# Split-weight matmuls of a two-layer decoder step: moving operands read backwards, weight rows of 136 columns, activation tiles at one offset from the weights

## What is computed

```python
def trunk_layer(x, ...):
    h = rmsnorm(x, norm1)
    qa, ka, va, hb, gate_b, gate_c, qc, fc, ic, og, zg = split_in(h @ w_in)   # 1024 -> 6400
    ya = dilated attention(rope(qa), rope(ka), va)      # six heads, three windows
    yb = gate_b * short convolution(gate_c * hb)
    yc = HGRN2 recurrence(qc, fc, ic), normed, times silu(og)
    g = sigmoid(zg + b_gate)
    mix = g[0] * (ya @ w_pa) + g[1] * (yb @ w_pb) + g[2] * (yc @ w_pc)
    x = x + mix @ w_o                                   # 1024 -> 1024
    h2 = rmsnorm(x, norm2)
    return x + square(relu(h2 @ w_up)) @ w_down, states # 1024 -> 4096 -> 1024
```

## Time and profile before

| | us |
|---|---|
| median of 3 runs | 812.23 (811.56 to 812.31) |
| span of the profiled execution, first to last instruction | 809.8 |
| TensorE matmuls busy | 801.3 (99%) |
| TensorE weight loads busy | 789.7 (98%) |
| VectorE busy | 570.3 (70%) |
| ScalarE busy | 439.6 (54%) |
| GpSimd busy | 274.7 (34%) |
| DMA packets, share of 16 engines (q1) | 72.3% |

### The profile page before, as it was taken

How to read it: one execution, slowest core, us unless ns; L and a number is a source line. 1 busy time by engine, 2 the same in 40 slices (tenths; PEclk the granted TensorE clock), 3 DMA queues, 4 the chain that set the end, 5 groups by cost and what they waited for, 6 DMA issues and landing times.

```text
span 809.8 us, 17686 instructions
## 1 busy us (share of the span) xinstructions
PE 801.3 (99%) x6786; PEld 789.7 (98%) x6786; DVE 570.3 (70%) x774; ACT 439.6 (54%) x627; POOL 274.7 (34%) x246
## 2 busy tenths in 40 slices
PE   8999999999999999999999999999999999999996
PEld 8999999999999999999999999999999999999996
DVE  6978898577877665545577788966797666645552
ACT  6663667545557664444354637674455666644442
POOL 3599293055700000122149827702663000001220
PEclk9999999999999999999999999999999999999998
DMA  8797779868567688777558968986765767787751
GB/s 327 226 342 279 279 236 328 229 226 314 185 208 226 215 287 285 257 239 250 190 179 225 359 244 289 278 254 232 271 225 178 247 235 250 240 285 241 253 207 53
DMA packets 125721, 199.88 MB, mean 247 GB/s; under 512 B 19680, under 2 KB 115376, under 8 KB 118192
## 3 DMA queue, kind: packets, MB, share of 16 engines
q1 hardware_dynamic: 124368, 196.48, 72.3%
q10 hardware_dynamic: 1296, 2.61, 0.9%
HBM read 191.17 MB, written 51.90 MB: 300 GB/s over the span
## 4 chain that ended last, share of the span: by engine, by line
PE 98%; DVE 1%; DMA 1%; ACT 0%; DVEq 0%; ACTq 0%; issue 0%
PE main L695 29%; PE main L696 28%; PE main L697 28%; PE small L697 1%; PE small L696 1%; PE small L695 1%; PE small L711 1%; PE small L740 1%; PE small L754 1%; DMA raw<-in_w_in 1%; PE main L680 1%; PE main L681 0%; PE main L684 0%; PE small L792 0%; PE main L671 0%; PE small L928 0%
## 5 line engine op out<-in xcount | busy, mean ns | idle before, releaser
L1043 ACT ACTIVATE w_hi<-raw 128x1024 fp32r<-128x1024 f32 (+1 forms) x256 | 266.4, 1043 | 234.3 <-PE main L697 148.6
L1292 DVE TENSOR_TENSOR w_lo<-raw,w_hi 128x1024 fp32r<-128x1024 f32 (+1 forms) x256 | 340.8, 1332 | 65.5 <-ACT w_hi L1043 64.5
L695 PE MATMUL main<-h_hi,w_hi 128*128 128x264 f32 x1248 | 357.9, 287 | 0.0
L696 PE MATMUL main<-h_lo,w_hi 128*128 128x264 f32 x1248 | 354.0, 284 | 0.0
L697 PE MATMUL main<-h_hi,w_lo 128*128 128x264 f32 x1248 | 353.9, 284 | 0.0
L695 PEld LDWEIGHTS main<-h_hi,w_hi 128*128 128x128 f32 x1248 | 235.3, 189 | 3.0 <-DVE w_lo L1292 1.5
L696 PEld LDWEIGHTS main<-h_lo,w_hi 128*128 128x128 f32 x1248 | 235.5, 189 | 0.1
L697 PEld LDWEIGHTS main<-h_hi,w_lo 128*128 128x128 f32 x1248 | 234.2, 188 | 0.0
L695 PE MATMUL main<-a_hi,w_hi 128*128 128x264 f32 x512 | 145.4, 284 | 0.0
L697 PE MATMUL main<-a_hi,w_lo 128*128 128x264 f32 x512 | 145.2, 284 | 0.0
L696 PE MATMUL main<-a_lo,w_hi 128*128 128x264 f32 x512 | 145.2, 284 | 0.0
(11 more groups left out here) (241 smaller groups left out, 1042.5 us busy)
## 6 DMA issues: line engine op xcount, KB each, us to landing
raw<-in_w_in SPq DMA_DIRECT2D x48, 1024.0 KB, 6.3
raw<-in_w_up SPq DMA_DIRECT2D x32, 1024.0 KB, 5.3
raw<-in_w_down SPq DMA_DIRECT2D x32, 1024.0 KB, 5.4
out_kvs<-in_cache SPq DMA_DIRECT2D x48, 512.0 KB
out_kvs<-in_cache SPq DMA_DIRECT2D x32, 496.0 KB
raw<-in_w_o SPq DMA_DIRECT2D x8, 1024.0 KB, 6.0
raw<-in_w_br SPq DMA_DIRECT2D x8, 768.0 KB, 4.8
gates<-q_scratch SPq DMA_DIRECT2D x4, 768.0 KB, 7.9
```

The lines of the kernel that those rows point to most:

```text
L695: pe.matmul(out[:, 0:TOK], wh, rh, start=start and k == 0, stop=False)
L696: pe.matmul(out[:, 0:TOK], wh, rl, start=False, stop=False)
L1043: act.activation(w_hi[:, slot(l, u), 0:k, :], raw_of(u, k), ACT.Copy).then_inc(w_hi_ready, 1)
L1292: dve.tensor_tensor(w_lo[:, slot(l, u), 0:k, :], raw_of(u, k), w_hi[:, slot(l, u), 0:k, :].bitcast(F32), ALU.subtract).then_inc(w_lo_ready, 1)
```

## The change

A helper `product` is put in place of `pe.matmul` in `first_units`, `unit_lo_last` and `unit`. It gives the same matmul with the moving operand's 264 columns from the last to the first and, so that the result lands where it did, the output's columns from the last to the first as well. The weights are loaded as before. Every block of `w_hi` and `w_lo` gets a row of 136 columns (544 bytes, of which 128 columns are used), so that its address moves on by 32 modulo 256 with each `k`, as the activations' does. Unused tiles (`before_h`, `before_gates`, `before_y_hi`, `before_y_lo`) put all activation tiles of the products (`h`, `mix`, `a`, `y`) at 64 modulo 256, which is 192 bytes on from the weights' 128. To make room, three small tiles that lay side by side share columns on different partitions (`sample_heads`). No instruction is added, dropped or moved, on any engine; operands and addresses differ.

```diff
+LINE = 8
-        w_hi = sb("w_hi", [P, RING, KT, P], F32R)
-        w_lo = sb("w_lo", [P, RING, KT, P], F32R)
+        w_hi_rows = sb("w_hi_rows", [P, RING, KT, P + LINE], F32R)
+        w_lo_rows = sb("w_lo_rows", [P, RING, KT, P + LINE], F32R)
         x = sb("x", [P, KT, TOK])
+        sb("before_h", [P, 6 * LINE])
         h_hi = sb("h_hi", [P, KT, TOK], F32R)
...
+        sb("before_gates", [P, 7 * LINE])
...
-            kv_s = sb("kv_s", [SAMPLES, NG, 2, P], stack=early)
-            q_s = sb("q_s", [SAMPLES, NG, P], stack=early)
+            sample_heads = sb("sample_heads", [P, NG * 2 * P], stack=early)
...
-            v_s = sb("v_s", [SAMPLES, 2, P], stack=early)
...
+            sb("before_y_hi", [P, 4 * LINE], stack=early)
             y_hi = sb("y_hi", [P, BT, TOK], F32R, stack=early)
+            sb("before_y_lo", [P, 2 * LINE], stack=early)
             y_lo = sb("y_lo", [P, BT, TOK], F32R, stack=early)
...
+        w_hi, w_lo = (t[:, :, :, 0:P] for t in (w_hi_rows, w_lo_rows))
+        kv_s = sample_heads[0:SAMPLES, :].rearrange("p (g k c) -> p g k c", g=NG, k=2)
+        v_s = sample_heads[32:32 + SAMPLES, 0:2 * P].rearrange("p (a c) -> p a c", a=2)
+        q_s = sample_heads[64:64 + SAMPLES, 0:NG * P].rearrange("p (g c) -> p g c", g=NG)
...
+            def product(out, w, rhs, start, stop):
+
+                return pe.matmul(out[:, TOK - 1::-1], w, rhs[:, ::-1], start=start, stop=stop)
...
-                    pe.matmul(out[:, 0:TOK], wh, rh, start=start and k == 0, stop=False)
-                    pe.matmul(out[:, 0:TOK], wh, rl, start=False, stop=False)
-                    last = pe.matmul(out[:, 0:TOK], wl, rh, start=False, stop=stop and k == nk - 1)
+                    product(out, wh, rh, start and k == 0, False)
+                    product(out, wh, rl, False, False)
+                    last = product(out, wl, rh, False, stop and k == nk - 1)
```

More of the change, by code:

```diff
@@ L665, in first_units @@
                         for u in us:
-                            pe.matmul(main[u][:, 0:TOK], w_hi[:, u, k, :], h_hi[:, k, :], start=k == 0, stop=False)
-                            pe.matmul(main[u][:, 0:TOK], w_hi[:, u, k, :], h_lo[:, k, :], start=False, stop=False)
+                            product(main[u], w_hi[:, u, k, :], h_hi[:, k, :], k == 0, False)
+                            product(main[u], w_hi[:, u, k, :], h_lo[:, k, :], False, False)
                     pe.wait_ge(piece_lo, i + 1)
@@ L670, in first_units @@
                         for k in ks:
-                            mm = pe.matmul(main[u][:, 0:TOK], w_lo[:, u, k, :], h_hi[:, k, :], start=False,
-                                           stop=k == KT - 1)
+                            mm = product(main[u], w_lo[:, u, k, :], h_hi[:, k, :], False, k == KT - 1)
                         if k == KT - 1:
@@ L679, in unit_lo_last @@
                 for k in range(KT):
-                    pe.matmul(out[:, 0:TOK], w_hi[:, u % RING, k, :], h_hi[:, k, :], start=k == 0, stop=False)
-                    pe.matmul(out[:, 0:TOK], w_hi[:, u % RING, k, :], h_lo[:, k, :], start=False, stop=False)
+                    product(out, w_hi[:, u % RING, k, :], h_hi[:, k, :], k == 0, False)
+                    product(out, w_hi[:, u % RING, k, :], h_lo[:, k, :], False, False)
                 pe.wait_ge(w_lo_ready, u + 5)
                 for k in range(KT):
-                    last = pe.matmul(out[:, 0:TOK], w_lo[:, u % RING, k, :], h_hi[:, k, :], start=False,
-                                     stop=k == KT - 1)
+                    last = product(out, w_lo[:, u % RING, k, :], h_hi[:, k, :], False, k == KT - 1)
                 return last
```

## The result

The change makes the kernel slower: 816.37 us in the median of five runs (815.77 to 816.70) against 811.84 for the kernel before on the same chip, a ratio of 1.0053 with a 95% interval of 1.0041 to 1.0066. The profiled execution spans 814.6 us, 4.8 more than before. The forecast was 783.

The account below looks back on a forecast made before the run. TensorE was taken as the bound, matmul count times distance. 32.7 us gained less 4 given back is 28.7; span 809.8 - 28.7 = 781.1, plus 2.4 for the median gives 783.5, say 783 us; range 762 to 814.

Parts of the forecast that it names:

- The bound: Whole kernel: TensorE busy 801.3 of 809.8 us, so time is the matmul count times the distance between starts.
- the 8.3 ns: Each split matmul: 120.8 ns less 112.5 for the stream, read as two on-chip memory reads getting in each other's way.
- Rows 6 and 7: Profile rows of weight loads beside one-column matmuls (about 110 ns each) and plain float32 matmuls of 264 columns (222.5 ns).
- the sum's term 6048 x (120.8 - 115.4) = 32.7 us: All matmuls but the first four units' 96: distance falls from 120.8 to 115.4 ns, saving 32.7 us.
- The rival "nothing": All matmuls: excess is a price of fp32r beside a weight load, same for any address; 812 us, chance 0.12.
- the 26 cycles: Each split matmul's cost beyond its 264 columns: 10.8 ns, 66 us over 6144 matmuls.
- The count of meetings: Moving read against weight load: 6.1 meetings per matmul at 1.36 ns now, 2.1 after, 2.9 ns, if weights are read downward.
- The end "one phase for all blocks": Equal pitches and offset 192: offset no longer averaged; distance from 112.5 ns at the good end to 121.1, no gain.
- weights read upward: Rival, all matmuls: reading backwards makes 2.1 meetings 6.1, distance 137 ns, 909 us; chance 0.12 by the weights' direction.
- The signs in the distances: Distances of 0.13 and 0.11 within one unit, branch units 121.7 ns against 120.8: weak sign of an address conflict.
- No cost for the splits and for backward writing of PSUM: ScalarE and VectorE splits stay at 1043 and 1332 ns a unit; backward output writes on TensorE cost nothing.
- The 4 us to be given back by a faster TensorE: Waits where weights come at DMA's pace, about 3 us, and at attention's VectorE splits, 1 us; 0 to 8.

Follow-up runs that it names:

- the best offset: Changed kernel with activations at offset 64 instead of 192 from the weights and all products read forwards: 805.39 us against 811.68, ratio 0.9922.
- Direction alone: Kernel before, addresses unchanged, with only the moving operands read and the outputs written backwards: 811.71 us against 811.91, ratio 0.9998.

## Why the prediction was wrong

**The bound** was read rightly: the time is the count of matmuls times their distance, and every kernel here bears it out (the span's 4.8 us are TensorE's 4.8 us).

**The step that failed** is the reading of the 8.3 ns. Rows 6 and 7 gave a floor of 112.5 ns for the stream and of 110 for the weight load, and from "neither gives 120.8" the prediction went to the two reads getting in each other's way. But none of those rows had a moving read that walks at one column a cycle: plain float32 takes two cycles a column (222.5 ns for 264), so its read walks at half the pace, and the load of the earlier trace rows had one moving column. The missing case, full pace without a full weight load, was the one that decided, and it costs 120.8 ns with 32 weight columns. The excess belonged to the walk of the moving read. So the sum's term 6048 x (120.8 - 115.4) = 32.7 us had nothing behind it; the best offset gave 6.3 us, the change's own took 4.5. The rival "nothing" held that the 26 cycles stay whatever the address; that was the truth for nearly all of them, and it had a chance of 0.12. Its reason, a price of fp32r beside a weight load, was not right either: with 32 weight columns the price is the same.

**The count of meetings** (6.1 against 2.1, 1.36 ns each) was arithmetic on a mechanism that no row showed. Direction alone: ratio 0.9998. In which direction weights are read was not tested by itself; nothing here needs it.

**The end "one phase for all blocks"** was seen: the forecast said that with both pitches equal the offset is no longer averaged and can fall well or badly. What was mis-sized is the scale. Its ends were 112.5 and 121.1 ns; measured are 119.7 to 124.6. The bad end was the one that counted, and it was put as "no gain" instead of a loss. A walk through all offsets mixes good and bad, so fixing the offset could from the start go either way around 120.8; this is the slower case that should have stood among the rivals. The one that stood there (weights read upward, 909 us) had the wrong mechanism and price.

**The signs in the distances**, uneven within a unit and dearer in the branches, were real signs of an address effect, but of the small one. (The 121.7 ns were read off rounded starts of the first unit of a pair; by the trace's starts the two units of a pair take 121.6 and 121.2.) An effect that is seen to vary by some ns was taken for the whole of the excess, which did not vary: `h`, `a` and `mix` all had 2.90 us a unit.

**No cost for the splits and for backward writing of PSUM**: right, 1042 and 1329 ns, and 0.9998. The 4 us to be given back by a faster TensorE could not be seen in the changed kernel, as it was not faster; in the kernel with offset 64 nearly all came through: 1.1 ns less in the mean distance over 6068 distances is 6.5 us, and 6.3 were gained.

## What to carry to other kernels

Before a cost is put down to a conflict of two streams, look for a row in which one of them runs at full pace without the other; where the trace has none, that is a probe to run first, and the forecast needs the case that the cost is one stream's own. Taking an average over many alignments down to one alignment is a draw, to be made by measuring all of them (here eight offsets and two directions, from 119.7 to 124.6 ns), and a pattern can hang on what ran just before, a small product or a wait of 0.14 us, so it is to be measured in the whole kernel.

## What was not expected of the hardware

- An fp32r moving operand is streamed at 0.449 ns a column when it walks through memory (264 to 512 columns), and at 0.417 when it stays within 8 columns; weights of 32, 64 or 128 columns make hardly a difference to it where the offset walks (120.8, 121.3 and 120.8 ns for 264 columns), up to 5.6 ns at one fixed offset.
- With a step of 2 columns a matmul of 264 columns takes 235.6 ns, about what reading the whole stretch of 527 would by the 0.449 ns (239).
- The same instructions at the same addresses run in one of two patterns, 120.3 or 122.5 ns a matmul, for up to 187 us on end. In the first layer one small product placed 0.36 us later changed the pattern; in the second a wait of 0.14 us did.
- At 128, 200 and 232 moving columns the weight load is the floor, 111.0, 111.3 and 111.7 ns for 128 weight columns. An estimate from 0.449 ns a column + 2.5 puts the crossing at some 240 columns.
